# Latents and weights split ahead, query outputs over three banks, and a new order of key-value, rotation and z chunks in a two-block kernel

## The reference

```python
h = rms_norm_2(x, g_mix[l]) * (1.0 + sc1) + sh1
proj = h @ w_in[l]
dn_qkv, dn_z, dn_b, dn_a, c_q, c_kv, k_r, gates = jnp.split(proj, split_at, axis=-1)
y_dn = gated_deltanet_branch(dn_qkv, dn_z, dn_b, dn_a, conv_w[l], a_log[l], dt_bias[l],
                             dn_o_gain[l]) @ w_o_dn[l]
y_mla = mla_branch(c_q, c_kv, k_r, q_gain[l], w_uq[l], kv_gain[l], w_ukv[l], cos, sin) @ w_o_mla[l]
```

## Time and profile before

| | us |
|---|---|
| median of 3 runs | 1761.75 |
| lowest and highest | 1761.55 and 1762.59 |
| the profiled execution | 1762.42 |
| its span | 1760.7 |

### The profile page before, as it was taken

How to read it: one execution, slowest core, us unless ns; L and a number is a source line. 1 busy time by engine, 2 the same in 40 slices (tenths; PEclk the granted TensorE clock), 3 DMA queues, 4 the chain that set the end, 5 groups by cost and what they waited for, 6 DMA issues and landing times.

```text
span 1760.7 us, 35255 instructions
## 1 busy us (share of the span) xinstructions
PE 1576.2 (90%) x14826; PEld 1309.9 (74%) x14826; DVE 864.9 (49%) x1248; ACT 661.4 (38%) x883; POOL 148.0 (8%) x188
## 2 busy tenths in 40 slices
PE   9999999999999999999989999899998666666677
PEld 8999899988989989998888898788985222222223
DVE  5765466646665546664567688966641000000001
ACT  5445355434544435542555744535442000000001
POOL 5800000000000000000105002130110000000000
PEclk9999999999999999999999999999999676777679
DMA  7755556765735666664444244002799999999997
GB/s 249 255 200 182 182 164 191 239 242 165 252 132 179 231 190 190 183 190 163 133 129 159 91 151 142 28 27 73 281 415 413 421 421 421 421 421 421 421 421 291
DMA packets 254141, 417.17 MB, mean 237 GB/s; under 512 B 15102, under 2 KB 215345, under 8 KB 229425
## 3 DMA queue, kind: packets, MB, share of 16 engines
q1 hardware_dynamic: 253825, 414.59, 65.7%
q10 hardware_dynamic: 176, 0.53, 0.1%
HBM read 414.04 MB, written 1.05 MB: 236 GB/s over the span
## 4 chain that ended last, share of the span: by engine, by line
issue 47%; PE 41%; DVE 4%; POOL 4%; ACT 3%; DMA 1%; DVEq 0%; SPq 0%; POOLq 0%; ACTq 0%
PE bank L426 4%; PE bank L427 4%; PE bank L428 4%; PE bank L1891 3%; PE bank L442 2%; PE bank L443 2%; PE bank L444 2%; PE bank L1081 1%; PE bank L1083 1%; PE bank L1082 1%; PE bank L454 1%; PE bank L761 1%; PE bank L455 1%; PE bank L456 1%; POOL ang L912 1%
## 5 line engine op out<-in xcount | busy, mean ns | idle before, releaser
L250 DVE TENSOR_TENSOR w_lo<-w_raw,w_hi 128x2048 fp32r<-128x2048 f32 (+2 forms) x178 | 401.3, 2257 | 254.3 <-ACT w_hi L243 250.5
L243 ACT ACTIVATE w_hi<-w_raw 128x2048 fp32r<-128x2048 f32 (+2 forms) x178 | 334.3, 1881 | 155.2 <-DMA w_raw<-in_ffn_w_down_dram 59.7
L426 PE MATMUL bank<-h_hi,w_hi 128*128 128x256 f32 x1168 | 325.8, 279 | 8.2 <-DVE h_lo L639 3.8
L427 PE MATMUL bank<-h_lo,w_hi 128*128 128x256 f32 x1168 | 324.7, 278 | 0.0
L428 PE MATMUL bank<-h_hi,w_lo 128*128 128x256 f32 x1168 | 324.7, 278 | 0.0
L2736 PE MATMUL bank<-w_exp,xeT 128*32 128x256 f32 x2048 | 170.8, 472 | 81.7 <-DMA w_exp<-in_w_up_dram 48.5
L426 PEld LDWEIGHTS bank<-h_hi,w_hi 128*128 128x128 f32 x1168 | 220.8, 189 | 9.8 <-issue 7.8
L428 PEld LDWEIGHTS bank<-h_hi,w_lo 128*128 128x128 f32 x1168 | 219.6, 188 | 0.0
L427 PEld LDWEIGHTS bank<-h_lo,w_hi 128*128 128x128 f32 x1168 | 219.4, 188 | 0.0
L2736 PEld LDWEIGHTS bank<-w_exp,xeT 128*32 128x32 f32 x2048 | 65.3, 127 | 177.9 <-DMA w_exp<-in_w_up_dram 83.0
L2736 PE MATMUL bank<-w_exp,hT 128*32 128x256 f32 x1024 | 94.1, 506 | 46.3 <-DMA w_exp<-in_w_down_dram 46.2
(11 more groups left out here) (539 smaller groups left out, 3084.3 us busy)
## 6 DMA issues: line engine op xcount, KB each, us to landing
w_exp<-in_w_gate_dram SPq DMA_DIRECT2D x64, 1024.0 KB, 26.7
w_exp<-in_w_up_dram SPq DMA_DIRECT2D x64, 1024.0 KB, 26.7
w_exp<-in_w_down_dram SPq DMA_DIRECT2D x64, 1024.0 KB, 26.8
w_raw<-in_ffn_w_gu_dram SPq DMA_DIRECT2D x88, 512.0 KB, 5.0
w_raw<-in_w_in_dram SPq DMA_DIRECT2D x54, 512.0 KB, 4.7
w_mod<-in_w_mod_dram SPq DMA_DIRECT2D x24, 1024.0 KB, 7.3
w_raw<-in_ffn_w_down_dram SPq DMA_DIRECT2D x44, 512.0 KB, 4.2
w_raw<-in_mem_w_kv_dram SPq DMA_DIRECT2D x32, 512.0 KB, 4.6
```

Source lines behind the costliest of these rows:

```text
L243: e.activation(whi[slot][:, 0:w], raw[slot][:, 0:w], ACT.Copy).then_inc(S["hi_ready"], 1)
L250: e.tensor_tensor(wlo[slot][:, 0:w], raw[slot][:, 0:w], whi[slot][:, 0:w].bitcast(F32), ALU.subtract).then_inc(S["lo_ready"], 1)
L426: e.matmul(dst, whi[slot][:, lo:hi_], bh[:, k, :], start=begin, stop=False)
L427: e.matmul(dst, whi[slot][:, lo:hi_], bl[:, k, :], start=False, stop=False)
```

## The change

The query latents are normalised and split (high, low) apart from the key-value latents and ahead of them. After the low part of the query latents, both splits of the first two query weight chunks (n + 2 and n + 3) are issued, ahead of the first convolution chunk; the key-value latents' gains come before that chunk's convolution, and their split and the third query chunk's (n + 4) after it. `gemm` leaves out what is listed in `split_ahead`. A square root on an unused cell is issued on ACT before the key's transposes. The memsets of `pad` move ahead of the latents' work. The query chunks use X[0], X[1], X[2]. They wait for the query latents alone. The four key-value chunks become single calls: the first, then the rotation of key and queries, the second, then z in one piece, then the third and fourth, then the third convolution chunk.

```diff
+    split_ahead = set()
     def first_split(m):
         act.raw(lambda e: hi_split(e, m, m % RING))
         dve.raw(lambda e: lo_split(e, m, m % RING))
+        split_ahead.add(m)
...
             m = base + c + AHEAD
-            if isinstance(c, int) and c + AHEAD >= n + follow:
+            if isinstance(c, int) and (c + AHEAD >= n + follow or m in split_ahead):
                 return
...
+        def clear(self):
+            for b in range(2):
+                for o_ in (0, SEQ + 2):
+                    self.tz = dve.do(lambda e, b=b, o_=o_: e.memset(pad[:, b, :, o_:o_ + 2], 0.0), *self.free)
...
+    act.do(lambda e: e.activation(small[:, 176:177], eps[:, 0:1], ACT.Sqrt), t_eps)
...
+    conv = [Conv(0, mod_done), None]
+    conv[0].clear()
+    roots_l = {}
     for j, (k0, k1) in enumerate(((0, 4), (4, 6))):
+        t2 = dve.do(lambda e, j=j, n_=(k1 - k0) * P: e.tensor_scalar(rl[:, j, :], X[j][:, 0:SEQ], 1.0 / n_, EPS, ALU.mult, ALU.add), sums_done[j], th)
         xfree[j] = t2
-        t3 = act.do(lambda e, j=j: e.activation(rl[:, j, :], rl[:, j, :], ACT.Sqrt), t2)
-        t3 = dve.do(lambda e, j=j: e.reciprocal(rl[:, j, :], rl[:, j, :]), t3)
+        roots_l[j] = act.do(lambda e, j=j: e.activation(rl[:, j, :], rl[:, j, :], ACT.Sqrt), t2)
...
+    inverse_length(0)
+    gained_latents(0, 0, 4)
+    t_hq = latents_hi(0, 0, 4)
+    inverse_length(1)
+    t_lq = latents_lo(0, 4, t_hq)
+    first_split(st.n + 2)
+    first_split(st.n + 3)
+
+    gained_latents(1, 4, 6)
     conv[0].chunk(0)
...
+    t_hk = latents_hi(1, 4, 6)
     t_krr = xfree[3] = act.do(lambda e: e.activation(krr[:, :], X[3][:, 0:SEQ], ACT.Copy), tp)
+    t_l = latents_lo(4, 6, t_hk)
+    first_split(st.n + 3)
     conv[0].chunk(1)
...
-        e.wait_ge(*(xfree_at[c] if c < 2 else (S["act_evac"], ea_uq + c - 1)))
+        e.wait_ge(*(xfree_at[c] if c < 3 else (S["act_evac"], ea_uq + c - 2)))
...
-        pairs.append((X[c % 2][:, 0:SEQ], lambda w, k: w[:, k, P:2 * P]))
+        pairs.append((X[c % 3][:, 0:SEQ], lambda w, k: w[:, k, P:2 * P]))
...
-    gemm(4, uq_source, uq_chunk, act_chunk=uq_evac, ready=[t_l], act_ready=[t_l], width=4 * 384,
+    gemm(4, uq_source, uq_chunk, act_chunk=uq_evac, ready=[t_lq], act_ready=[t_l], width=4 * 384,
...
+        free_of_b = xfree[b]
+        gemm(1, cols(A["w_ukv_2"][0], width=512, first=c * 512), chunk, act_chunk=evac, ready=[t_l], width=2 * BANK)
+        xfree[b] = act_evacs()
+    ukv(0, 3)
     t_kz = pool.do(lambda e: e.memset(krz[0][64:128, :], 0.0), t_l)
...
-    t_q = rope_fm(qr, 4, rope2, swap2, P, [t_ukv, t_swap2], xn_rope)
+    t_q = rope_fm(qr, 4, rope2, swap2, P, [t_uq, t_swap2], xn_rope)
     t_rope2 = t_q
-    for _ in z_side:
+    ukv(1, 3)
+    for _ in z_part(0):
         pass
+    ukv(2, 2)
+    ukv(3, 3)
+    t_ukv = act_evacs()
     conv[0].chunk(2)
```

More of the change, by code:

```diff
@@ L1400, in silu_of @@
             e.activation(self.fin[c // 2][:, (c % 2) * 2:(c % 2) * 2 + 2, :], cy[:, c % 2, :, :], ACT.Silu).then_inc(conv_silu, 1)
+        def clear(self):
+            for b in range(2):
+                for o_ in (0, SEQ + 2):
+                    self.tz = dve.do(lambda e, b=b, o_=o_: e.memset(pad[:, b, :, o_:o_ + 2], 0.0), *self.free)
         def chunk(self, c, in_parts=False):
[L1404 to L1407, removed]
+            if c == 0 and self.tz is None:
+                self.clear()
             self.padded[c] = (S["act_evac"], st.evac_a + 1)
@@ L1508, in build @@
     t_ab = xfree[2] = act.do(lambda e: e.activation(ab[:, :, :], x3[:, :, 64:96], ACT.Copy), tp)
+    conv = [Conv(0, mod_done), None]
+    conv[0].clear()
+    roots_l = {}
     for j, (k0, k1) in enumerate(((0, 4), (4, 6))):
-        tp = sums_done[j]
-        t2 = dve.do(lambda e, j=j, n_=(k1 - k0) * P: e.tensor_scalar(rl[:, j, :], X[j][:, 0:SEQ], 1.0 / n_, EPS, ALU.mult, ALU.add), tp, th)
+        t2 = dve.do(lambda e, j=j, n_=(k1 - k0) * P: e.tensor_scalar(rl[:, j, :], X[j][:, 0:SEQ], 1.0 / n_, EPS, ALU.mult, ALU.add), sums_done[j], th)
@@ L1512, in build, with inverse_length, gained_latents @@
         xfree[j] = t2
-        t3 = act.do(lambda e, j=j: e.activation(rl[:, j, :], rl[:, j, :], ACT.Sqrt), t2)
-        t3 = dve.do(lambda e, j=j: e.reciprocal(rl[:, j, :], rl[:, j, :]), t3)
+        roots_l[j] = act.do(lambda e, j=j: e.activation(rl[:, j, :], rl[:, j, :], ACT.Sqrt), t2)
+    inv_l, gained_l = {}, {}
+    def inverse_length(j):
+        inv_l[j] = dve.do(lambda e: e.reciprocal(rl[:, j, :], rl[:, j, :]), roots_l[j])
+    def gained_latents(j, k0, k1):
         for k in range(k0, k1):
@@ L1516, in build @@
             g_ = col("q_gain_2", k) if j == 0 else col("kv_gain_2", k - 4)
[L1517 to L1522, removed]
+            gained_l[j] = dve.do(lambda e, k=k, g_=g_: e.scalar_tensor_tensor(
+                out=lat[:, k, :], in0=lat[:, k, :], scalar=g_, in1=rl[:, j, :], op0=ALU.mult, op1=ALU.mult), inv_l[j])
@@ new lines, in latents_hi, with latents_lo @@
+    def latents_hi(j, k0, k1):
+        return act.do(lambda e: e.activation(a_hi[:, 8 + k0:8 + k1, :], lat[:, k0:k1, :], ACT.Copy), gained_l[j])
+    def latents_lo(k0, k1, t_hi):
+        return dve.do(lambda e: e.tensor_tensor(a_lo[:, 8 + k0:8 + k1, :], lat[:, k0:k1, :], a_hi[:, 8 + k0:8 + k1, :].bitcast(F32),
+                                                ALU.subtract), t_hi)
+    inverse_length(0)
[3 more added lines that the diff above has]
+    t_lq = latents_lo(0, 4, t_hq)
@@ L1544, in uq_evac @@
         e.activation(qn[:, 2 * c:2 * c + 2, :], G[u][:, :].rearrange("p (h t) -> p h t", h=2), ACT.Copy)
-        return e.activation(qr[:, c, :], X[c % 2][:, 0:SEQ], ACT.Copy)
+        return e.activation(qr[:, c, :], X[c % 3][:, 0:SEQ], ACT.Copy)
     xfree_at = dict(xfree)
@@ L1565, in build @@
     also_in.update({uq0 + c: (rotated_in[c], 16) for c in range(4)})
-    gemm(4, uq_source, uq_chunk, act_chunk=uq_evac, ready=[t_l], act_ready=[t_l], width=4 * 384,
+    gemm(4, uq_source, uq_chunk, act_chunk=uq_evac, ready=[t_lq], act_ready=[t_l], width=4 * 384,
          beside={c: uq_rotated(c) for c in range(4)})
[L1570 to L1599, removed]
+    t_uq = act_evacs()
@@ new lines, in build, with ukv, chunk, evac @@
+    for b in range(3):
+        xfree[b] = t_uq
+    def ukv(c, b):
+        def chunk(e, c_, u, slot):
+            e.wait_ge(*free_of_b)
+            for hh in range(2):
+                dst = G[u][:, hh * SEQ:(hh + 1) * SEQ]
+                for k in range(2):
+                    a_ = k * BANK + hh * 256
+                    w0, w1 = whi[slot][:, a_:a_ + P], wlo[slot][:, a_:a_ + P]
+                    e.matmul(dst, w0, a_hi[:, 12 + k, :], start=(k == 0), stop=False)
+                    e.matmul(dst, w0, a_lo[:, 12 + k, :], start=False, stop=False)
+                    e.matmul(dst, w1, a_hi[:, 12 + k, :], start=False, stop=(k == 1))
+            for t_ in range(TT):
+                dst = X[b][:, t_ * 256:(t_ + 1) * 256]
+                xs = slice(t_ * P, (t_ + 1) * P)
+                for k in range(2):
+                    w0, w1 = (w[slot][:, k * BANK:(k + 1) * BANK].rearrange("p (h n) -> p h n", h=2)[:, :, P:2 * P] for w in (whi, wlo))
+                    e.matmul(dst, a_hi[:, 12 + k, xs], w0, start=(k == 0), stop=False)
+                    e.matmul(dst, a_hi[:, 12 + k, xs], w1, start=False, stop=False)
+                    ins = e.matmul(dst, a_lo[:, 12 + k, xs], w0, start=False, stop=(k == 1))
+            return ins
+        def evac(e, c_, u, ch):
+            e.activation(kn[:, 2 * c:2 * c + 2, :], G[u][:, :].rearrange("p (h t) -> p h t", h=2), ACT.Copy)
+            return e.activation(vm[:, :, c * 256:(c + 1) * 256], X[b][:, :].rearrange("p (t n) -> p t n", t=TT), ACT.Copy)
+        free_of_b = xfree[b]
+        gemm(1, cols(A["w_ukv_2"][0], width=512, first=c * 512), chunk, act_chunk=evac, ready=[t_l], width=2 * BANK)
+        xfree[b] = act_evacs()
```

## The result

The kernel after takes 0.9947 of the time of before (95% interval 0.9928 to 0.9966), 9.3 us less, where 6.6 us had been forecast. Its profiled execution took 1755.93 us, its span is 1754.2 us, 6.5 us shorter than the span in the earlier trace rows.

The account below looks back on a forecast made before the run. The changed stretch was taken as bound by PE's and DVE's queues, with PE idle in four gaps. Query gaps 5.4 + z 1.3 - heads 0.1 = 6.6 us, off the 1761.75 us median: 1755.1 us, range 1753.5 to 1758.4.

Parts of the forecast that it names:

- the four gaps close: PE's idle 4.8 us ahead of three query chunks and 1.1 us ahead of z would go.
- PE asks for query chunks when said: PE would need the four query weight chunks at 896.1, 900.4, 904.7 and 908.9 us.
- z's load is in time: Ahead of z: load landed at 914.0 us, split by 918.3, wanted at 920.9; its gap goes, saving 1.3 us.
- the masks matter to nobody: GpSimd's masks move 20 us ahead, beside DVE's splits; cost taken as 0.
- the third bank is worth 0: At query chunk 2, a third bank saves between 0 and 0.3 us; taken as 0.
- the load at the entry to the heads does not move ahead: Released at 929.6 us against 929.8 before, split by 938.9 or 940.1; PE loses 0.1 us, bounds 0 and 0.5.
- the gain travels to the end: Behind 945 us, a gain made in the changed stretch should carry through to the kernel's end.
- rivals (b) to (e): Heads swallow the gain, 9%; late z landing slows it, 3%; masks and rotation moved gain more, 8%; faulty change, unpriced.
- Rival (a): DVE becomes the bound at the query chunks, with 0.7 us of cover: 1756.1 to 1758.2 us; chance 14%.
- (918.63 - 910.08) / 2 = 4.27 us each: PE's time per query chunk, from the last two, which run without a gap in the profile of before.
- The term of 5.4 us for the three gaps: Ahead of query chunks 0 to 2: 3.1, 1.1 and 1.2 us saved, together 5.4 us.
- the rest of the stretch, forecast to shrink by 1.2 us: Behind the query chunks: 1.3 us saved at z's gap, less 0.1 us lost at the heads.

Follow-up runs that it names:

- `k0_null`: The kernel before, unchanged, timed against itself; ratio 0.9994 (0.9979 to 1.0009).
- `x8_before`: The kernel before, unchanged, executed once more for a profile only; 60.5 us from key to heads, no ratio formed.
- `x1_filled`: The kernel before with unread products put into PE's four gaps, nothing reordered; ratio 1.0007 (0.9992 to 1.0022).
- `x2_busy`: The kernel after with 56 unread products (6.6 us) on PE where the gaps had been; ratio 1.0009 (0.9990 to 1.0027) of before.
- rear half: The kernel before up to the query chunks, with two query banks, and the new order behind them; ratio 0.9990, again 0.9986.
- front half: Latents in two parts, splits and table load ahead, three banks; key-value chunks, rotation and z in the order of before; ratio 0.9949, again 0.9966.
- masks late: The kernel after with GpSimd's masks held back until the third convolution chunk has been copied; ratio 0.9968 (0.9950 to 0.9986) to before.
- two banks: The kernel after with two query banks in turn instead of three; ratio 0.9961 (0.9942 to 0.9979) to before.

## Why the prediction was right in its mechanism and short in its size

Stretches from the key's first turning product to the first head score, by kernel (the two kernels that open a gap on purpose, without the table load and with DVE loaded, are left out):

| kernel | us | gaps in the query chunks | mean |
|---|---|---|---|
| before, `k0_null`, `x8_before` | 60.2, 60.5, 60.5 | open | 60.4 |
| `x1_filled`, `x2_busy` | 60.7, 59.6 | filled | 60.1 |
| rear half, twice | 58.2, 58.2 | open, z closed | 58.2 |
| front half, twice | 53.8, 54.7 | closed, z open | 54.3 |
| after (4), masks late, two banks (2) | 53.4, 52.1, 52.1, 52.1, 53.4, 53.4, 52.1 | closed | 52.7 |

Before minus the last row is 7.7 us on the means, not 6.6. That is 0.44%, a ratio of 0.9956. The kernel after alone has a mean of 52.4 us, which makes 8.0.

**Right**, by the steps of the prediction: the four gaps close; PE asks for query chunks when said; z's load is in time; the masks matter to nobody as far as runs can tell; the third bank is worth 0; the load at the entry to the heads does not move ahead and PE does not notice; the gain travels to the end (the times from the heads' start to the router's load, 301.3 to 302.9 us before and 301.2 to 302.2 us after, overlap). None of the rivals (b) to (e) came about. Rival (a) is close: the cover is 1.3 us at the slow pace and 0.7 at the quick one, and without the table load it is used up.

**The step that failed** is the sum's use of one profile's pace, "(918.63 - 910.08) / 2 = 4.27 us each", for a gain that is the difference of two stretches with different bounds. Before, DVE times query chunks 0 to 2 and a transfer times z; a quicker PE only waits longer: the third query chunk begins 25.7 us behind the key's first turning product whatever the pace ahead of it, and the first key-value chunk at 34.2. After, PE times all of it, and a quick pace is cashed: the first key-value chunk begins at 28.7 us in the first profile (914.04 less 885.35) and at 27.9 us in the three quick ones, and the heads at 53.4 and 52.1 us. The term of 5.4 us for the three gaps measured 5.6 and 6.4 us; the rest of the stretch, forecast to shrink by 1.2 us, shrank by 1.2 us in the first pair and by up to 2.0. So the gain is 6.8 us when both are as in the profile of before, and up to 8.4 us (60.5 - 52.1) when the pace is quick. The second part of the shortfall is that the profile of before was the cheapest of three: 60.15 against 60.5 us. In the two dearer ones the clock had fallen behind the first gap, but that is not what cost the 0.35 us: up to the first key-value chunk all three agree to 0.02 us (34.24, 34.23 and 34.25). They part behind it, at ACT's high splits that wait for a landing. Timelines of ACT in `k0_null` and `x8_before`:

```profile
933.10 1.92 ACT L243 ACTIVATE w_hi<-w_raw 128x2048 fp32r<-128x2048 f32 x1 [1.48 <-DMA w_raw<-in_w_in_dram]
```

```profile
932.74 1.92 ACT L243 ACTIVATE w_hi<-w_raw 128x2048 fp32r<-128x2048 f32 x1 [1.39 <-DMA w_raw<-in_w_in_dram]
```

Both stand 46.96 us behind the key's first turning product; the same split in the profile of before stands at 930.99, which is 46.60 us behind it. That the first pair of profiles agreed with the sum so closely was luck in this sense: it paired the cheapest execution of before with the one execution of the kernel after, of four, that had the slow pace.

**The range** failed with it. It was made of bounds on the steps, 1753.5 to 1758.4 us, while the measured ratio put on the median of before is 1761.75 x 0.9947 = 1752.4 us. The 7.7 us of the stretches, at 1754.1, would lie inside. What was not in the range at all is the spread between executions, which puts about 3.5 us to each side on a comparison of this size; the prediction names that figure below its sum and leaves it out of its bounds.

**What stays open.** The kernel after alone gives 9.3 us (7.6 to 11.1), its four profiles 8.0 us. All six comparisons of kernels without a gap (after four times, masks late, two banks) give 0.9953 weighted, with 0.0008 to each side, or 8.2 us, which agrees with 7.7. Pooling the masks and the banks with after rests on their profiles showing no difference. The halves give 0.9959 and 0.9988, together 9.3 us, while their stretches are shorter by 6.1 and 2.2 us, together 8.3: the rear half cashes pace as well, since a quick PE after its last gap no longer waits for z. The profiles show no surplus behind the stretch: from the first head score to the end of the span are 814.1 to 816.8 us in the three profiles of before and 815.0 to 818.4 in the four of the kernel after. One of up to 1.5 us is neither shown nor excluded by the times. And what sets PE's pace to 0.113 or 0.118 us in an execution is unknown.

No version here beats the kernel after: in the changed stretch there is no gap left to close.

## What to carry to other kernels

Price a closed gap as the difference of two bounds, not as the idle time of one profile: while another engine sets the time, whatever makes the waiting engine quicker is hidden in the gap, and closing it cashes that too. Read stretches from a common landmark in several profiles before believing a difference of whole spans; here 13 us of spread lay ahead of the change. Putting unread work in place of the idle time, in both kernels, tells whether the idle time itself is what is gained.

## What was not expected of the hardware

PE's like products stand 0.118 us or 0.113 us apart at the same granted clock of 1.00 (147 or 153 in 17 us), in long stretches that differ between executions of one program. Behind 3 us of idleness the granted clock fell in four of five profiles (0.66 over the next 5 us in `k0_null`), and the third query chunk began no later for it (25.67 to 25.69 us after the key's first turning product in all five).

Beside GpSimd's masks DVE's low split keeps its 2.29 us in the kernel after too, and GpSimd is the one that is held up: four selects take 3.97 us, while the six just ahead of them, with no such split beside them, took 1.18 us. Which of the two began first can't be read from a merged row. Timelines of DVE and POOL, kernel after:

```profile
930.18 2.29 DVE L250 TENSOR_TENSOR w_lo<-w_raw,w_hi 128x2048 fp32r<-128x2048 f32 x1 [2.69 <-ACT w_hi L243]
...
929.37 3.97 POOL L1685 TENSOR_SCALAR_AFFINE_SELECT msk<-msk 64x64 f32<-64x64 f32 x4
```
